# Small loads on ScalarE's queue, and the first transposes of x tile by tile over six PSUM banks

## What is computed

```python
h = rmsnorm(x, g_mix);  proj = h @ w_in          # q, k, v, GLU input, gates
o = diff_attention(q, k, v, lam, rel_bias)       # 4 heads, chunk-causal, relative bias
y_attn = (rmsnorm(o, g_subln) * (1 - lam_init)) @ w_attn_up
u = glu[:, :512] * sigmoid(glu[:, 512:])
u = silu(layernorm(causal_depthwise_conv(u, w_dw, b_dw), g_conv_ln, b_conv_ln))
y_conv = u @ w_conv_pw2 + b_conv_pw2
x = x + (gate_a * y_attn + gate_b * y_conv) @ w_out
x = x + hier_moe(rmsnorm(x, g_ffn), ...)         # 64 experts, top 2 of 8 in the top group
return rmsnorm(x, g_final)
```

## Time and profile before

| what | value |
|---|---|
| median of three runs | 1259.97 us (1259.83 to 1260.48) |
| profiled execution | 1260.33 us |
| its span, first to last instruction | 1258.5 us |
| mean granted TensorE clock | 0.962 |
| TensorE busy | 1121.8 us (89%) |
| VectorE, ScalarE, GpSimd busy | 563.0, 271.3, 143.0 us |
| DMA | 408.83 MB, mean 325 GB/s |

### The profile page before, as it was taken

The page is one execution under the profiler, slowest core; times in us unless marked ns, Lnnn a source line. Parts: engine busy times, 40 slices in busy tenths (PEclk is TensorE's granted clock), DMA queues, the critical chain, the costliest instruction groups (busy, mean ns, idle before and its releaser), DMA issues.

```text
span 1258.5 us, 29959 instructions
## 1 busy us (share of the span) xinstructions
PE 1121.8 (89%) x12401; PEld 689.0 (55%) x12402; DVE 563.0 (45%) x1176; ACT 271.3 (22%) x683; POOL 143.0 (11%) x84
## 2 busy tenths in 40 slices
PE   5999999989999988679997999997998867896877
PEld 4878777768884544335553555554554434453435
DVE  3799433445245543234443444443443333342441
ACT  4133234385132111111111111111111111111112
POOL 2454543156100000000000000000000000000000
PEclk9999999999999998889998999998999988898989
DMA  6333111153159999998999999999999999999994
GB/s 236 118 101 111 67 67 68 68 201 121 80 216 368 421 424 425 427 425 365 412 427 426 426 425 423 425 425 428 425 425 425 426 424 425 425 427 425 426 423 191
DMA packets 51309, 408.83 MB, mean 325 GB/s; under 512 B 6410, under 2 KB 6567, under 8 KB 21066
## 3 DMA queue, kind: packets, MB, share of 16 engines
q1 hardware_dynamic: 50778, 407.22, 78.2%
q0 software_dynamic: 352, 1.06, 0.3%
q10 hardware_dynamic: 144, 0.07, 0.0%
HBM read 406.22 MB, written 2.11 MB: 324 GB/s over the span
## 4 chain that ended last, share of the span: by engine, by line
DMA 60%; PE 33%; ACT 3%; DVE 2%; issue 1%; SPq 1%; DVEq 0%; ACTq 0%
DMA sb_weights<-in_w_exp_up 55%; PE ps_all L1492 12%; PE ps_all L1736 4%; DMA sb_weights<-in_w_exp_gate 3%; PE ps_all L1795 2%; PE ps_all L1543 2%; PE ps_all L1749 1%; PE ps_all L1717 1%; PE ps_all L1670 1%; PE ps_all L1674 1%; PE ps_all L1667 1%; DMA sb_consts<-in_consts 1%; PE ps_all L1622 1%; PE ps_all L1625 1%; PE ps_all L1628 1%
## 5 line engine op out<-in xcount | busy, mean ns | idle before, releaser
L1736 PE MATMUL ps_all<-sb_weights,sb_late 128*32 128x256 f32 x4608 | 306.2, 420 | 88.0 <-DMA sb_weights<-in_w_exp_up 86.5
L1736 PEld LDWEIGHTS ps_all<-sb_weights,sb_late 128*32 128x32 f32 x4608 | 168.3, 117 | 217.2 <-issue 131.6
L1397 DVE TENSOR_TENSOR sb_late<-sb_late,ps_all 128x128 f32<-128x128 f32 x72 | 20.7, 288 | 395.2 <-ACT sb_late L970 395.2
L1392 DVE TENSOR_TENSOR sb_x<-sb_x,ps_all 128x512 f32<-128x512 f32 x184 | 114.1, 682 | 105.0 <-PE ps_all L1795 105.0
L1749 PE MATMUL ps_all<-sb_weights,sb_late 128*32 128x256 f32 x2304 | 140.4, 384 | 0.4 <-ACT sb_late L974 0.4
L1717 PE MATMUL ps_all<-sb_hT,sb_late 128*32 128x256 f32 x2304 | 138.4, 380 | 0.6 <-DVE sb_late L1266 0.6
L1492 PE MATMUL ps_all<-sb_hT_r,sb_ring_r 128*128 128x512 f32 x512 | 124.1, 394 | 0.0
L1492 PEld LDWEIGHTS ps_all<-sb_hT_r,sb_ring_r 128*128 128x128 f32 x512 | 94.8, 188 | 26.8 <-issue 6.5
L1717 PEld LDWEIGHTS ps_all<-sb_hT,sb_late 128*32 128x32 f32 x2304 | 75.5, 109 | 61.2 <-issue 17.4
L1749 PEld LDWEIGHTS ps_all<-sb_weights,sb_late 128*32 128x32 f32 x2304 | 67.9, 110 | 64.3 <-issue 27.0
L970 ACT ACTIVATE sb_late<-ps_all 128x128 f32<-128x128 f32 x72 | 20.0, 278 | 368.0 <-PE ps_all L1736 368.0
(11 more groups left out here) (307 smaller groups left out, 1068.2 us busy)
## 6 DMA issues: line engine op xcount, KB each, us to landing
sb_weights<-in_w_exp_up SPq DMA_DIRECT2D x59, 2048.0 KB, 14.6
sb_weights<-in_w_exp_down SPq DMA_DIRECT2D x59, 2048.0 KB, 14.5
sb_weights<-in_w_exp_gate SPq DMA_DIRECT2D x59, 2048.0 KB, 14.5
sb_ring<-in_w_in SPq DMA_DIRECT2D x9, 2048.0 KB, 9.2
sb_x<-in_x SPq DMA_DIRECT2D x8, 512.0 KB, 5.0
sb_ring<-in_w_conv_pw SPq DMA_DIRECT2D x1, 2048.0 KB, 9.0
sb_ring<-in_w_attn_up SPq DMA_DIRECT2D x1, 2048.0 KB, 7.9
sb_ring<-in_w_out SPq DMA_DIRECT2D x1, 2048.0 KB, 12.8
```

The costliest lines, as they stand in the source:

```text
L1392: ins = dve.tensor_tensor(rows, rows, banks[g].rearrange("p (t s) -> p t s", t=T), ALU.add)
L1736: last = mm(ps_gu[g * BLK:(g + 1) * BLK, 0:2 * P].rearrange("p (a n) -> p a n", a=2), rows, weights[:, at:at + 3:2, r % 4, cols], start=r ...
```

## The change

`in_small` now counts the six vectors and the taps, and their seven loads are issued by ScalarE, behind the identity. `rel_bias` stays with SP, directly behind x, on a semaphore of its own (`in_rb`). The eight `xT` tiles leave the plan of rotating banks; the parts of the transpose get fixed banks (`hx_bank`), six different ones for c = 0 to 5, the first two again for 6 and 7. Parts 0 to 5 are transposed tile by tile of x, so that all six are completed with tile 3; parts 6 and 7 follow when part 0 or 1 has been lowered (`hT_lowered`). VectorE copies vectors and taps between the scalings of x tiles 1 and 2. The bias products stand behind all transposes and wait for `rel_bias` and for five lowered parts. Since eight tiles left the plan, every later tile sits one bank further.

```diff
@@ plan @@
     tiles = [("vec", 0)]
-    tiles += [("xT", c) for c in range(KD)]
     tiles += GLU + [("strip", h) for h in range(HEADS)]
@@ banks and semaphores @@
+        hx_bank = [ps_t, ps_o, ps_oT, ps_s[:, 0, :], ps_s[:, 1, :], bank[2], ps_t, ps_o]
+        in_rb, hx_done, hT_lowered = sem("in_rb"), sem("hx_done"), sem("hT_lowered")
@@ SP @@
-            at = 0
-            for name, rows in VEC_ROWS:
...
-                sp.dma_start(rows29[at:at + rows, :], ap(src)[0].rearrange("(r p) -> r p", p=P)).then_inc(in_small, 16)
-                at += rows
-            sp.dma_start(taps_row, ap("w_dw")[0]).then_inc(in_small, 16)
-            sp.dma_start(rb_sb[:, :], ap("rel_bias")).then_inc(in_small, 16)
+            sp.dma_start(rb_sb[:, :], ap("rel_bias")).then_inc(in_rb, 16)
@@ ScalarE @@
             act_e.dma_start(consts[:, 0:P], ap("consts")[:, 0:P]).then_inc(in_const, 16)
+            at = 0
+            for name, rows in VEC_ROWS:
...
+                act_e.dma_start(rows29[at:at + rows, :], ap(src)[0].rearrange("(r p) -> r p", p=P)).then_inc(in_small, 16)
+                at += rows
+            act_e.dma_start(taps_row, ap("w_dw")[0]).then_inc(in_small, 16)
...
             for c in range(KD):
-                tile_ready(act_e, "xT", c)
-                act_e.activation(hT[:, c, :], bank_of("xT", c)[:, :], ACT.Copy,
+                act_e.wait_ge(hx_done, c + 1)
+                act_e.activation(hT[:, c, :], hx_bank[c], ACT.Copy,
@@ VectorE @@
             square_x(2)
-            for t in range(1, T):
-                scale_x(t)
-
+            scale_x(1)
             tile_ready(dve, "vec", 0)
             link(dve.tensor_copy(vec[:, :], bank_of("vec", 0)[:, 0:NVEC]))
...
+            for t in range(2, T):
+                scale_x(t)
             for c in range(KD):
                 dve.wait_ge(hT_high, c + 1)
-                dve.scalar_tensor_tensor(out=hT_low[:, c, :], in0=bank_of("xT", c)[:, :],
+                dve.scalar_tensor_tensor(out=hT_low[:, c, :], in0=hx_bank[c],
...
-                                         op0=ALU.mult, op1=ALU.subtract).then_inc(copied("xT", c), 1)
+                                         op0=ALU.mult, op1=ALU.subtract).then_inc(hT_lowered, 1)
@@ TensorE, split_columns @@
                 dst = open_tile(kind, m)
+                if n == 1:
+                    pe.wait_ge(hT_lowered, KD)
...
                         if n == 0 and i == 2:
-                            tile_out(pe, "xT", c)
+                            pe.wait_ge(hT_lowered, c + 1)
@@ TensorE, head @@
-            pe.wait_ge(in_small, 16 * (len(VEC_ROWS) + 2))
+            pe.wait_ge(in_small, 16 * (len(VEC_ROWS) + 1))
...
                 pe.wait_ge(in_const2, 16)
+                pe.wait_ge(in_rb, 16)
+                pe.wait_ge(hT_lowered, 5)
...
-            first = [open_tile("xT", c) for c in range(2)]
             for t in range(T):
                 pe.wait_ge(xn_ready, t + 1)
-                for c in range(2):
-                    last = pe.transpose(first[c][:, t * P:(t + 1) * P], xn[:, t, c * P:(c + 1) * P], ident)
+                for c in range(6):
+                    last = pe.transpose(hx_bank[c][:, t * P:(t + 1) * P], xn[:, t, c * P:(c + 1) * P], ident)
                     if t == T - 1:
-                        last.then_inc(tile_done, 1)
-            for c in range(2, KD):
-                dst = open_tile("xT", c)
+                        last.then_inc(hx_done, 1)
+            for c in range(6, KD):
+                pe.wait_ge(hT_lowered, c - 5)
                 for t in range(T):
-                    last = pe.transpose(dst[:, t * P:(t + 1) * P], xn[:, t, c * P:(c + 1) * P], ident)
-                last.then_inc(tile_done, 1)
-                if c == 5:
-                    bias_rows()
+                    last = pe.transpose(hx_bank[c][:, t * P:(t + 1) * P], xn[:, t, c * P:(c + 1) * P], ident)
+                last.then_inc(hx_done, 1)
+            bias_rows()
```

More of the change, by code:

```diff
@@ L568, in _ @@
                 sp.dma_start(x[:, t, :], ap("x")[0, t * P:(t + 1) * P, :]).then_inc(in_x[t], 16)
-            at = 0
-            for name, rows in VEC_ROWS:
-                src = {"g_mix": "g_mix", "b_pw2": "b_conv_pw2", "b_dw": "b_dw", "g_ln": "g_conv_ln",
-                       "b_ln": "b_conv_ln", "g_sub": "g_subln"}[name]
-                sp.dma_start(rows29[at:at + rows, :], ap(src)[0].rearrange("(r p) -> r p", p=P)).then_inc(in_small, 16)
-                at += rows
-            sp.dma_start(taps_row, ap("w_dw")[0]).then_inc(in_small, 16)
-            sp.dma_start(rb_sb[:, :], ap("rel_bias")).then_inc(in_small, 16)
+            sp.dma_start(rb_sb[:, :], ap("rel_bias")).then_inc(in_rb, 16)
             for n, name in enumerate(CHUNKS):
@@ L751, in _ @@
             act_e.dma_start(consts[:, 0:P], ap("consts")[:, 0:P]).then_inc(in_const, 16)
+            at = 0
+            for name, rows in VEC_ROWS:
+                src = {"g_mix": "g_mix", "b_pw2": "b_conv_pw2", "b_dw": "b_dw", "g_ln": "g_conv_ln",
+                       "b_ln": "b_conv_ln", "g_sub": "g_subln"}[name]
+                act_e.dma_start(rows29[at:at + rows, :], ap(src)[0].rearrange("(r p) -> r p", p=P)).then_inc(in_small, 16)
+                at += rows
+            act_e.dma_start(taps_row, ap("w_dw")[0]).then_inc(in_small, 16)
             act_e.wait_ge(eps_set, 1)
```

## The result

The changed kernel takes 1265.68 us (median of 5 runs, 1264.31 to 1267.75) against 1259.97 for the kernel before: the ratio is 1.0042, with a 95% interval of 1.0031 to 1.0053, so it is slower by 3.9 to 6.7 us. Its profiled execution took 1264.31 us with a span of 1262.5 and a mean granted TensorE clock of 0.964. The forecast of 1261.9 was wrong, and so was its range, which ended at 1264.2.

A forecast was written before the change was run, and what follows sets the result against it. Expert-weight DMA (60%) and TensorE (33%) were untouched, so the head decided: the first projection matmul at 23.55 against 21.30, +2.25, taken as +1.9. That gave 1262.2 us profiled, 1261.9 median; range 1258.4 to 1264.2.

The forecast's parts named there:

- V: TensorE's first transpose, when vectors and taps have landed; forecast at 12.36 us, no change, with 13.5 as upper bound.
- The 10 for the last tile of x: Landing of the last x tile, forecast at about 10 us in place of 8.45 through packets alternating with the taps.
- G: Start of the first projection matmul; forecast at 23.55 us against 21.30 before.
- M: Start of ScalarE's weight copy: the later of the glu_b landing and V+6.85; forecast at 19.2 us.
- +1.9: Forecast delay of the first projection matmul in us, taken between +2.25 and +1.7, the latter with some faster transposes.
- deep batch: First transposes over six banks: first bank complete with the 19th, delayed 2.5 us, only 0.52 covered by glu_b's wait.
- Copies between the scalings: VectorE copies the vectors before scaling x tiles 2 and 3; claimed free, as TensorE is still at tiles 0 and 1.
- Rival (c): Cold start: TensorE's pause before the bias products slows the first tile by 1.5 us; +3.4, 1263.4; chance 0.18 including slow issues.
- L does not move: Landing of the first weights (glu_b) stays at 17.22 us, because one engine carries the whole taps load.
- rival (b): Place in SP's queue delays glu_b; issued earlier it lands at 14.8, G = 19.8, -1.5, 1258.5 us; chance 0.12.
- One for one to the end: A shift of the first projection matmul passes fully to the kernel's end; about 2.1 us of room to move forward.
- C: VectorE's first product on a GLU tile, named with the results: 38.12 us before, 43.20 in the changed kernel.

The follow-up runs named there:

- e3: The changed kernel with only transpose parts 0 and 1 tile by tile and the others part by part: 1263.01 us, ratio 1.0021 to the kernel before.
- e7: e3 with VectorE scaling x tiles 2 and 3 ahead of the copies of vectors and taps: 1260.87 us, ratio 1.0002 to the kernel before.
- e10: The changed kernel, six-bank order kept, with x tiles 2 and 3 scaled ahead of the copies: 1264.84 us, ratio 1.0035 to the kernel before.
- e2: The changed kernel with twelve extra identity transposes, four ahead of parts 6 and 7, eight ahead of the bias products: 1264.27 us, ratio 1.0028.
- after_again: The changed kernel run once more without any edit, beside the experiments: 1265.54 us, ratio 1.0040 to the kernel before.
- e5: The kernel before with only the seven small loads moved to ScalarE, rel_bias on its own semaphore: 1260.60 us, ratio 1.0000.
- e6: The kernel before with the taps loaded by two transfers of 16 and 15 rows, still by SP: 1260.12 us, ratio 0.9993.
- e1: The changed kernel with the taps loaded by two transfers of 16 and 15 rows: 1262.84 us, ratio 1.0016 to the kernel before.
- e9: e7 with taps in two loads of 16 and 15 rows and bias products behind the first GLU tile: 1258.28 us, ratio 0.9984.
- e4: The changed kernel with the seven small loads given back to SP: 1265.89 us, ratio 1.0040 to the kernel before.

## Why the prediction was wrong

**V, the step that failed first.** I took "12.36, no change", with 13.5 as the upper end. It is 13.63, and 13.36 to 14.88 over nine profiles. I had let the taps packets alternate with x on their engine from 4.6 us on, so that 18 of them were through by 9.0. In the trace of after the first of them starts at 7.88, not near 4.6, and only nine have started by 9.0; the others took turns with glu_b. The packets of the six vectors, which stand ahead of the taps in ScalarE's queue, go by between 3.9 and 7.56, and the last packet of x starts at 8.03. From the first 4.5 us of the earlier trace rows, where ScalarE's packets kept pace with SP's, I had extended a rule of sharing to the taps and given no time to the vectors ahead of them. Whether the vectors or x held the taps up, no run separates. The 10 for the last tile of x fell for the same reason (8.63). Issue time was never the question: ScalarE's seven issues ended at 3.8, the table load stood at 3.83, near the forecast, and cost nothing.

**V to G, right.** I had V+5.0 for the first high part and M+4.35 for G, with M the start of the high parts plus 1.85. Measured: V+5.04, and G = M+4.40 from the weight copy at M = 20.39. V to G is 11.16, and 23.55 less 12.36 was 11.19. But I then took +1.9 for a sum of +2.25, for transposes at the faster rate; measured without V it is +2.22. The deep batch costs what was said, e3 and e7 take it back, and the wait for glu_b went as forecast. The chain also went as forecast through VectorE's fifth lowering, which sets the bias products.

**Copies between the scalings, right at no cost, and by the reason given.** e10 shows it, and e3 the other half of the sentence: where TensorE comes to the later tiles early, it meets the scalings, for about 1.2 in the trace.

**The cold start, placed wrong and priced right in part by luck.** Rival (c) had 1.5 for matmuls at the slow spacing; the first tile lost 1.59 in after, and e2 gives it back. The price came from 3.5 us at the slow spacing, read off the first twelve transposes. But in the kernel before the next ones went on at 0.21 until 18.57, which makes 6.2 us from V; by that length the price would have been higher. In after the clock was low from 25.3 to 28.7, and in after_again for twice as long, at a loss of 3.2. What failed is that I made it an alternative to the forecast, with the forecast's own sum kept free of it. The pause of 2 us that feeds it is a part of the forecast's own path (M+3.15 against the end of the transposes), so whoever forecasts the deep batch forecasts this pause as well. Its price belonged into the upper end of the forecast at least. Measured, V to G (+2.22), V (+1.27) and the tile (+1.59) add up to the 5.08 at C; each of the three stood in the prediction, and no case there held more than two.

**"L does not move", wrong, without a cost.** I set the single engine against the place in SP's queue, as forecast against rival (b). Both are true, for about 1 us each: the move alone brings glu_b to 16.3 (e5), the split alone to 16.24 (e6), and both together to 15.2 in e1 and 14.7 in e9, where (b) had said 14.8. In after it landed at 3.16+13.3 = 16.5. But L was nowhere the later of the two inputs once the deep batch stood on V, so this gain of 0.7 met nothing. With V at 9.75, and without the deep batch, e9 got what (b) had described: G at 16.72, ahead of (b)'s 19.8, because the bias products had moved too.

**One for one to the end, right.** C +5.08, attention's output weights +5.03, span +4.0, median +5.7. The 1 to 2 us between a profile and the runs' median go with the mean granted clock, and 0.72 of them is found in the two traces (the first section); where the rest arises stays open.

## What to carry to other kernels

Pipelining with deeper batches delays the first result: before six banks are filled in an order that completes them together, count when the first consumer can start, and ask whether a pause that this opens in TensorE leads to a lower granted clock behind it. A small load that gates the start, with a number of rows like the 31 here, is worth cutting so that its rows divide well, and this paid here more than any change of who issues it. When costs are worked out as rival cases, check whether the forecast's own path produces the rival's condition; if so they are a sum.

## What the runs showed of the hardware

- A load of 62 KB on 31 rows, issued by ScalarE near 3.6, landed at 13.4 to 14.9, one packet for each 0.17 us while SP's queue was busy; as 16 and 15 rows it landed at 9.75 and 10.34. Behind SP's x it landed at 12.0 to 12.4. To have a queue to itself was no advantage against a place ahead of a 2 MB load.
- The granted clock fell to 0.50 within or behind pauses of 1.15 (e6) and 2.1 us (after, after_again, e1, e4, e10) in a stretch of scattered transposes, and stayed there for some 3 to 7 us, most of it dense matmuls. It did not fall behind one of 0.73 (e3) or of 1.73 (e7), nor in e2, whose twelve extra transposes cut the pause to 1.24. The Trainium skill (TensorE: Matmul & The Clock Gate, Part 1) has an idle array fall from 2.4 to 1.2 GHz and says that the number of slow matmuls varies from run to run of one kernel; the two profiles of the changed kernel, with first tiles of 6.93 and 7.50, agree.
- The 24 transposes in a row took from 4.19 to 5.38 us in seven profiles, with a granted clock of 1.00 written beside all of them. That column can't be believed there: in every profile the transposes start each 0.21 us up to one moment and each 0.11 us behind it (14.8 in e1, 18.4 in after, 18.6 before, 20.1 in after_again), and in each the first entry that the trace holds for the clock stands at this same moment. So TensorE worked at half rate, which is the lower of its two levels (1.2 GHz), from V until then, for 3.5 (e4) to 6.7 us (e3).
